# A two-part transformer block on one core: where value products, decays and root steps stand in three attention stages

## The reference, cut to what matters

```python
def mla_mixer(h, ...):                      # first attention, 8 heads, 256 tokens
    proj = h @ w_in                         # c_q 384, c_kv 256, k_pe 64
    q  = (rms_norm(c_q, q_a_norm) @ w_uq)   # 8 heads x (128 + 64)
    kv = (rms_norm(c_kv, kv_a_norm) @ w_ukv)# 8 heads x (128 keys + 128 values)
    q_nope, k_nope = rms_norm(...), rms_norm(...)        # per head
    q_pe, k_pe = rope(rms_norm(...)), rope(rms_norm(...))
    logits = (q_nope @ k_nope.T + q_pe @ k_pe.T) * scale # causal
    return softmax(logits) @ v @ w_o

def moba_mixer(h, w_qkv, ...):              # second attention, 8 heads of 128
    q, k, v = split(h @ w_qkv)
    q, k = rms_norm(q, q_norm), rms_norm(k, k_norm)      # per head
    return softmax(q @ k.T * scale + rel_bias) @ v @ w_o

def first_block(x, ...):
    x = x + mla_mixer(norm(x)); x = x + sq_relu_mlp(norm(x))
    x = x + moba_mixer(norm(x)); x = x + sq_relu_mlp(norm(x))

def hybrid_layer(x, ctx, ...):              # third stage: both halves side by side
    attn = neighbourhood_attention(q, k, v, kc, vc, rpb, rows)   # 8 heads of 64
    y    = ssd_bidirectional(...)  # decay = exp(cum_i - cum_j), masked, times C B^T dt
    x = x + gate * (concat(attn, y) @ w_out); x = x + gate * conv_glu(...)
```

## Time and profile before

| | |
|---|---|
| runs of the kernel | 1105.79, 1106.78, 1111.33 us (median 1106.78) |
| the profiled execution | 1100.91 us, of it span 1099.3 us |
| busy: PE / DVE / ACT / POOL | 94% / 64% / 48% / 9% |
| chain that ended last | PE 74%, DVE 13%, ACT 6%, issue 3%, DMA 2% |
| mean granted TensorE clock | 0.983 of 2.4 GHz |

### The profile page before, as it was taken

How to read it: one execution, slowest core, us unless ns; L and a number is a source line. 1 busy time by engine, 2 the same in 40 slices (tenths; PEclk the granted TensorE clock), 3 DMA queues, 4 the chain that set the end, 5 groups by cost and what they waited for, 6 DMA issues and landing times.

```text
span 1099.3 us, 15596 instructions
## 1 busy us (share of the span) xinstructions
PE 1036.1 (94%) x6112; PEld 886.9 (81%) x6112; DVE 703.4 (64%) x946; ACT 529.1 (48%) x712; POOL 99.2 (9%) x77
## 2 busy tenths in 40 slices
PE   7989899999999997989999999999999889999996
PEld 5556789888997875889999887988966678999995
DVE  5645556888736556557676754456477477777774
ACT  2463447766444557444554543553344255445442
POOL 0120004665000010000000000000000000000000
PEclk9997999999999999999999999999999999999998
DMA  8034466767643551547777542334100145445531
GB/s 351 1 126 104 153 232 251 274 241 272 255 158 115 191 191 44 219 159 269 280 281 283 198 184 78 115 118 151 39 1 1 43 175 200 176 172 186 200 148 57
DMA packets 29725, 183.89 MB, mean 167 GB/s; under 512 B 3440, under 2 KB 6128, under 8 KB 10096
## 3 DMA queue, kind: packets, MB, share of 16 engines
q1 hardware_dynamic: 25216, 156.84, 39.2%
q0 software_dynamic: 3456, 25.17, 6.5%
q10 hardware_dynamic: 1008, 1.27, 0.3%
HBM read 180.64 MB, written 2.62 MB: 167 GB/s over the span
## 4 chain that ended last, share of the span: by engine, by line
PE 74%; DVE 13%; ACT 6%; issue 3%; DMA 2%; POOL 1%; ACTq 0%; DVEq 0%; SPq 0%
PE bank L662 20%; PE bank L663 19%; PE bank L664 19%; DVE split L1795 4%; ACT split L1297 4%; PE bank L857 3%; PE bank L671 2%; DMA consts<-in_consts 2%; PE bank L1162 2%; PE bank L1143 1%; PE bank L945 1%; POOL stat L593 1%; PE bank L804 1%; DMA raw<-w_mlp 1%; ACT arena L1298 1%
## 5 line engine op out<-in xcount | busy, mean ns | idle before, releaser
L1795 DVE TENSOR_TENSOR split<-raw,split 128x2048 fp32r<-128x2048 f32 (+1 forms) x123 | 283.7, 2307 | 240.1 <-ACT split L1297 234.5
L1297 ACT ACTIVATE split<-raw 128x2048 fp32r<-128x2048 f32 (+1 forms) x123 | 233.6, 1899 | 267.7 <-PE bank L664 244.9
L662 PE MATMUL bank<-acts,split 128*128 128x256 f32 (+1 forms) x1024 | 290.6, 284 | 2.7 <-DVE acts L1833 1.4
L663 PE MATMUL bank<-acts,split 128*128 128x256 f32 (+1 forms) x1024 | 289.6, 283 | 0.0
L664 PE MATMUL bank<-acts,split 128*128 128x256 f32 (+1 forms) x1024 | 289.6, 283 | 0.0
L662 PE MATMUL bank<-split,acts 128*128 128x512 f32 (+1 forms) x544 | 214.4, 394 | 15.4 <-DVE split L1795 8.3
L663 PE MATMUL bank<-split,acts 128*128 128x512 f32 (+1 forms) x544 | 210.4, 387 | 0.0
L664 PE MATMUL bank<-split,acts 128*128 128x512 f32 (+1 forms) x544 | 210.3, 386 | 0.0
L662 PEld LDWEIGHTS bank<-acts,split 128*128 128x128 f32 (+1 forms) x1024 | 194.7, 190 | 6.2 <-issue 3.3
L663 PEld LDWEIGHTS bank<-acts,split 128*128 128x128 f32 (+1 forms) x1024 | 194.7, 190 | 2.3
L664 PEld LDWEIGHTS bank<-acts,split 128*128 128x128 f32 (+1 forms) x1024 | 194.7, 190 | 0.4
(11 more groups left out here) (245 smaller groups left out, 1189.6 us busy)
## 6 DMA issues: line engine op xcount, KB each, us to landing
raw<-w_mlp SPq DMA_DIRECT2D x64, 1024.0 KB, 4.9
raw<-w_glu SPq DMA_DIRECT2D x22, 1024.0 KB, 5.3
work<-w_ada POOLq DMA_DIRECT2D x12, 1024.0 KB, 5.1
raw<-w_qkv SPq DMA_DIRECT2D x12, 1024.0 KB, 4.8
bias<-w_ada POOLq DMA_DIRECT2D x12, 1024.0 KB, 5.1
arena<-w_glu_down SPq DMA_DIRECT2D x22, 512.0 KB, 3.3
raw<-w_mla_o SPq DMA_DIRECT2D x4, 1024.0 KB, 5.7
raw<-w_moba_o SPq DMA_DIRECT2D x4, 1024.0 KB, 4.8
```

What stands on the lines that cost most here:

```text
L662: pe.matmul(out_, a[0], b[0], start=first, stop=False)
L663: pe.matmul(out_, a[0], b[1], start=False, stop=False)
L1297: return act.activation(out_, in_, ACT.Copy)
L1795: v.tensor_tensor(split[:, c % 2, 1, 0:n], raw[:, c % 2, 0:n], split[:, c % 2, 0, 0:n].bitcast(F32), ALU.subtract).then_inc(lo_ready, 1)
```

## The change

What stays the same: every product, every weight byte, the four banks' turns. What changes:

1. **att0.** The four value units of `mla_ukv` are spread: one between the rotary q and the k transposes, one behind the k transposes, one behind S2, one behind O0. ACT's evictions follow (`values_out`, `beside0`). The rounded part of `mla_o` chunk 0 is made by DVE instead of ACT.
2. **Rotary keys.** `kpT` becomes two tiles of 128 rows, one with zeros in its lower and one in its upper half; L921 and L923 take 128 rows. POOL writes the zeros, ACT evicts the keys in two 64-row copies.
3. **att1.** The roots are taken in halves (q, then k; 16 columns each) and the loop covers q and k only. PE transposes q, makes value chunks 8 and 9, transposes k, makes the first half of chunk 10, S0 to S2, the other half, and chunk 11's halves behind O0 and O1. The splits of the chunks 12 and 13 (`moba_o` 0 and 1) move into and behind the attention.
4. **Third stage.** A step's segment (G, K, F) stands directly behind P, ahead of S, Y and O.

```diff
-            kpT = view(arena, 12288, T)
+            kpT = view(arena, 12288, T), view(arena, 12800, T)
@@ grid_order
         steps.append(("P", i))
+        steps.extend(x for x in SEGMENTS if SEGMENT_STEP.get(x) == i)
         ...
-        steps.extend(x for x in SEGMENTS if SEGMENT_STEP.get(x) == i)
@@ POOL
-            roots(0, 7)
+            roots(0, 3)
+            pool.wait_ge(roots_ready, 3)
+            pool.memset(kpT[0][64:128], 0.0).then_inc(kpe_zeros, 1)
+            pool.wait_ge(kpe_zeros, 1)
+            pool.memset(kpT[1][0:64], 0.0).then_inc(kpe_zeros, 1)
+            pool.wait_ge(kpe_zeros, 2)
+            roots(3, 7)
@@ PE, first attention
-            ukv_products(1)
             pe.wait_ge(heads_normed, 3)
             ...
+            ukv_products(1, 0)
             (k transposes)
+            ukv_products(1, 1)
+            def beside0(kind, h):
+                if (kind, h) == ("S", 2):
+                    ukv_products(1, 2)
+                    for u in range(4, 6):
+                        gemm_gone(pe, GU["mla_ukv"] + u)
+                if (kind, h) == ("O", 0):
+                    ukv_products(1, 3)
@@ scores0
-                pe.matmul(b[:, 0:T], qpT[a:a + 64, h // 2, P:T], kpT[a:a + 64, :], start=False, stop=True)
+                pe.matmul(b[:, 0:T], qpT[:, h // 2, P:T], kpT[h % 2][:, :], start=False, stop=True)
@@ PE, second attention
-            with pe.Fori(0, 3) as i:
+            with pe.Fori(0, 2) as i:
             ...
+            pe.wait_ge(heads_normed, 6)
+            for n in range(4):
+                heads_flip(n)
+            for c in range(2):
+                for t in range(2):
+                    value_products(c, t)
+            pe.wait_ge(heads_normed, 7)
+            for n in range(4, 8):
+                heads_flip(n)
+            value_products(2, 0)
+            def beside1(kind, h):
+                if (kind, h) == ("S", 2):
+                    value_products(2, 1)
+                    ...
+                if (kind, h) in (("O", 0), ("O", 1)):
+                    value_products(3, h)
@@ ACT
-            small_empty(SU["kpe"], kpT, T)
+            copy(kpT[0][0:64], sbank(SU["kpe"])[0:64, 0:T])
+            copy(kpT[1][64:128], sbank(SU["kpe"])[64:128, 0:T]).then_inc(small_free[SU["kpe"] % 4], 1)
-            split_hi(GC["mla_o"])
+            def beside0(h):
+                if h < 2:
+                    values_out(6 + h)
+            def beside1(h):
+                if h == 1:
+                    used(c0 + 10)
+                if h in (2, 3):
+                    values_out1(h)
+            causal_attention("att1", H, beside1)
+            used(c0 + 11)
@@ DVE
+            v.wait_ge(w_loaded[0], 16)
+            v.tensor_copy(split[:, 0, 0, :], raw[:, 0, :]).then_inc(hi_ready, 1)
             split_lo(GC["mla_o"])
@@ DVE, second attention
-            inverse_rms(8, [(32, P)])
+                    if (i, j) == (1, 1):
+                        heads_scaled(0)
+                means_of(8 + 16 * i, [(16, P)])
+            heads_scaled(1)
+            def beside1(h):
+                if h == 3:
+                    used(GC["qkv"] + 10)
```

More of the change, by code:

```diff
@@ L621, in _ @@
                 ada_load(j, att)
-            roots(8, 10)
+            roots(8, 11)
             pool.wait_ge(small_ready, SU["att1"] + 24)
@@ L626, in _ @@
                 ada_load(j, bias)
-            roots(10, 12)
+            roots(11, 13)
             for j in range(14, 24):
@@ L630, in _ @@
                 ada_load(j, bias)
-            roots(12, 13)
+            roots(13, 14)
             pool.memset(cum_rows, 0.0).then_inc(zeros_ready, 1)
@@ L638, in _ @@
             pool.wait_ge(zeros_ready, 3)
-            roots(13, len(ROOTS))
+            roots(14, len(ROOTS))
         @block.tensor
@@ L806, in t5_products, with causal_attention @@
                     ins.then_inc(small_ready, 1)
-            def causal_attention(name, scores, value, count):
+            def causal_attention(name, scores, value, count, beside):
                 for kind, h in seq_c:
@@ L825, in causal_attention @@
                             .then_inc(small_ready, 1)
+                    beside(kind, h)
             pe.wait_ge(ident_in_sb, 16)
@@ L1504, in causal_attention @@
                         transposed(h - 1)
-            causal_attention("att0", 0)
+                    beside(h)
+            def beside0(h):
+                if h < 2:
+                    values_out(6 + h)
+            causal_attention("att0", 0, beside0)
             split_hi(GC["mla_o"] + 1)
@@ L1561, in _, with values_out1 @@
                             .then_inc(gemm_free[u % 4], 1)
-            for j in range(4):
-                used(c0 + 8 + j)
-                for m in range(j - 1, j + 1) if j % 2 else ():
-                    empty(u0 + 8 + m, qkv[:, m % 2, 2048 + 512 * (m // 2):2560 + 512 * (m // 2)],
-                          scale=stat[:, m % 2:m % 2 + 1])
             for n in range(4):
                 pair_empty(SU["q1"] + n, pair(q1T, n), col("moba_q"))
+            def values_out1(n):
+                empty(u0 + 8 + n, qkv[:, n % 2, 2048 + 512 * (n // 2):2560 + 512 * (n // 2)], scale=stat[:, n % 2:n % 2 + 1])
+            used(c0 + 8)
+            used(c0 + 9)
+            values_out1(0)
+            values_out1(1)
             for n in range(4):
                 pair_empty(SU["k1"] + n, pair(k1T, n), col("moba_k"))
-            causal_attention("att1", H)
+            def beside1(h):
[5 more added lines that the diff above has]
+            used(c0 + 11)
             project_and_cols("moba_o", "m1")
@@ L1582, in _ @@
                 two_hi("hc", m, 1)
[L1583 removed]
+            norm_second_tile(14)
             used(GC["mlp1"] + 31)
@@ L2121, in _, with causal_attention @@
             scale_k_nope(1)
+            v.wait_ge(w_loaded[0], 16)
+            v.tensor_copy(split[:, 0, 0, :], raw[:, 0, :]).then_inc(hi_ready, 1)
             split_lo(GC["mla_o"])
-            def causal_attention(name, scale, bias_of, count):
+            def causal_attention(name, scale, bias_of, count, beside=None):
                 def logits(h):
@@ L2160, in causal_attention @@
                         normalise(h - 1)
+                    if beside:
+                        beside(h)
             causal_attention("att0", 1.0 / math.sqrt(NOPE + ROPE), lambda h: const("causal"), 0)
@@ L2250, in _, with heads_scaled @@
             means_of_x(2)
-            with v.Fori(0, 2) as i:
+            def heads_scaled(n):
+                v.wait_ge(roots_ready, 10 + n)
+                for u in range(4 * n, 4 * n + 4):
+                    gemm_gone(v, GU["qkv"] + u)
+                for t in range(2):
+                    qk = qkv[:, t, D * n:D * (n + 1)].rearrange("p (h d) -> p h d", d=P)
+                    at = 8 + 16 * n + 8 * t
+                    ins = v.tensor_tensor(qk, qk, spread(stat[:, at:at + 8], 1, P), ALU.mult)
+                    if t:
+                        ins.then_inc(heads_normed, 1)
+                    else:
+                        step(ins)
@@ L2252, in _ @@
+            for i in range(2):
                 for j in range(4):
-                    used(GC["qkv"] + j, i, 4)
+                    used(GC["qkv"] + 4 * i + j)
                     for m in range(j - 1, j + 1) if j % 2 else ():
-                        v.wait_ge(sq_ready, 4 * i + (11 + m))
+                        v.wait_ge(sq_ready, 4 * i + 11 + m)
                         sq = att[:, 512 * (m % 2):512 * (m % 2) + 512].rearrange("p (a b) -> p a b", a=4)
-                        v.tensor_reduce(stat[:, bass.ds(8 * i + (8 + 16 * (m % 2) + 4 * (m // 2)), 4)], sq, AX.X,
-                                        ALU.add).then_inc(sq_used, 1)
@@ L2260, in _ @@
-            used(GC["qkv"] + 8)
-            v.wait_ge(sq_used, 18)
-            inverse_rms(8, [(32, P)])
-            for u in range(8):
-                gemm_gone(v, GU["qkv"] + u)
-            for t in range(2):
-                used(GC["qkv"] + 9 + t)
-                qk = qkv[:, t, 0:2 * D].rearrange("p (h d) -> p h d", d=P)
-                ins = v.tensor_tensor(qk, qk, spread(stat[:, 8 + 16 * t:24 + 16 * t], 1, P), ALU.mult)
-                if t:
-                    ins.then_inc(heads_normed, 1)
-                else:
-                    step(ins)
+                        at = 8 + 16 * i + 8 * (m % 2) + 4 * (m // 2)
```

88 lines of the change are left out of this document (57 added, 31 removed).

## The result

| | before | after |
|---|---|---|
| runs of the pair, us | 1102.68 to 1111.33 (median 1106.28 of 4) | 1071.38 to 1077.66 (median 1075.1 of 4) |
| profiled execution / span, us | 1100.91 / 1099.3 | 1072.88 / 1071.3 |
| mean granted TensorE clock | 0.983 | 0.992 |
| busy PE / DVE / ACT | 94% / 64% / 48% | 95% / 66% / 49% |

The ratio is 0.9712, with a 95% interval of 0.966 to 0.9764: the changed kernel is faster by 31 us on this chip. Beside the experiments it was timed on two more chips: 1074.47 against 1103.18 (ratio 0.9739, interval 0.9699 to 0.9779) and 1075.03 against 1102.71 (0.9733, 0.9713 to 0.9753), so by 28 to 29 us there. 1081 was forecast, with 1074 to 1090 as range; all three medians (1075.1, 1074.47, 1075.03) lie in the range, but under the 1077 to 1084 that the prediction gave its own mechanism.

What follows compares the result with a forecast made beforehand. PE, busy 94% of the span with 74% of the chain, was taken as the bound, with idle or half-clock stretches to recover. Gains 15.8 (att0) + 7.2 (att1) + 2.9 (third stage) = 25.9 us; 1106.8 - 25.9 = 1080.9, stated 1081, range 1074 to 1090.

Steps and rivals of the forecast that it cites:

- its own mechanism: Whole kernel: the forecast's summed gains as laid out, 1081 us with own range 1077 to 1084, chance 0.55.
- the bounds 1.30 and 1.99: att0 scores per head: 1.30 us if padded to full height, 1.99 if unchanged; 1.30 was taken.
- att0's list: att0: PE's new order laid end to end from 66.9 us, projection at 100.7, gain 15.8 us.
- The waits at O0 and O1: att0: new PE waits on ACT, whose value copies stand behind exponentials, 0.6 and 0.9 us.
- The main assumption: att0: the clock is 1.00 all through, as PE has no gap over 1 us from 66.9 on.
- what preceded the fall is gone: att0: argument against the clock falling all the same; the idle 1.32 and 2.31 us are covered.
- rival B: att0: the clock falls all the same, for 17 us as before; its 8.5 us come back, 1089; chance 0.14.
- 8.5 + 3.6 + 5.5 less waits: att0 cross-check: half rate 8.5, idle time 3.6, shorter scores 5.5, less 1.5 of new waits: 16.1 us.
- The gain of 7.2: att1: PE's new list from 385.70 to the projection at 431.4, instead of 438.56; gain 7.2 us.
- The tail moves with it: Third stage: the tail, P14 on DVE on ACT on O5, moves with the stage's 2.9 us gain.
- the median of the runs is 5.9 higher: Last step: median 1106.8 against profiled 1100.9 before, so 1080.9 rather than 1075.0 is forecast.
- the low end allows for the low stretches of the slower runs going too: Range 1074 to 1090: its low end covers low-clock stretches of slower runs also disappearing.

Runs made afterwards that it cites:

- experiments 1 and 3: 1: changed kernel with one rotary key copy and 64-row rotary products, 1081.3 us. 3, first run: that kernel, second score pair turned round, 1074.69 us.
- Experiment 2: Kernel before with only the padding: rotary keys in two copies of 128 rows, no filling; 1092.41 us (ratio 0.9889).
- experiment 7: Changed kernel with waits in both attentions and the third stage attacked by order alone: 1067.93 and 1068.64 us; third stage's part alone 1070.14 us.
- the second run of experiment 3: Kernel before with only the second pair of score products in the other order, two shape changes a head instead of four; 1100.39 us (0.9976).
- short hole: Kernel before with the rounded part of the first `mla_o` chunk made on VectorE, no padding or filling; one run of 1094.75 us.
- experiment 5: Changed kernel with the third stage's order as before, segments last in their steps; 1079.56 us (0.9785).

## Why the prediction was right

**What bounds the kernel.** A stretch in which PE was busy at half clock, holes of PE in both attentions, and three waits in the third stage: each stage gave what its rows said, within 0.3 us.

**Scores.** Of the bounds 1.30 and 1.99 the lower was right, 1.31. The 0.69 was the shape, by experiments 1 and 3, and more exactly the change between shapes.

**att0's list.** S0 at 73.31 (laid at 73.0), the fourth value unit at 81.81 (81.6), P5 at 93.57 (93.8), projection at 100.48 (100.7). The waits at O0 and O1 are there with the releaser named, but 0.29 and 0.57 instead of 0.6 and 0.9; a head takes 2.29 and not 2.4, since an output product held PE for 0.65 and not the 0.76 of the earlier trace rows, which has a change of shape ahead of it too.

**The clock.** The main assumption held: 1.00 from 67.15 to 100.48. Its reason ("what preceded the fall is gone") is half of the story. Experiment 2 shows that most of what the low stretch cost, 5.1 of its 8.5 us, hung on the 64-row products (or the changes beside them) as well, which the prediction took for a matter of rate alone. Had the filling failed, the padding would have saved most of it, and rival B (1089, "as long a low stretch as before") was mispriced: a fall inside padded heads lasted 6.8 us and so costs 3.4, not 8.5. The check "8.5 + 3.6 + 5.5 less waits" came out right because either edit removes the shared part.

**Moved splits and queues.** The rounded copy on DVE took 1.23 us, near the lower bound, and ended with the subtraction at 72.2, ahead of the first logits at 74.82: zero. `mla_o` 2 was issued at 96.57; ACT began its split of that chunk at 107.81, released by PE and not by the DMA: zero, as said.

**att1.** From chunk 7's end: S0 18.5 us (forecast 18.4), P0 23.3 (23.1), P2 32.5 (32.1), P4 36.6 (36.4), projection 45.8 (45.7). S0's wait is 1.19 (0.9), O3's 0.19 (0.7). The gain of 7.2 was 7.06.

**Third stage.** 3.12 for 2.9: the three waits, and 0.2 us more. DVE waits for the outputs of a pair as foreseen, but for 5.2 us at O1 and O3 where 1 to 2 were put down, and not wholly within its slack: experiment 7 gets 0.6 us back ahead of P13 by moving `pair_lo`. "The tail moves with it" was right: P14's 2.61 stayed. It was not the fixed chain as which it was treated, though: experiment 7 removes it by moving the remainders of a pair (DVE) and one rounded pair (ACT).

**The sum and the median.** 26.2 us by the three marks against 25.9, and the forecast from the profiled execution, 1075.0, is 2.1 us over the measured 1072.88; 1.7 of these are the stretch at half clock at 860 us. The median came to 1075.1, 5.9 under the forecast and 1.9 under the forecast's own range, and the step that was off is the last one, "the median of the runs is 5.9 higher", with the same 5.9 added to the new kernel. (1 - clock) x span, averaged over the runs of a chip, is 22 to 23 us for the kernel before and 10 to 11 for the changed one. On the two chips that timed both side by side 13 and 10 us of clock loss went, not the 8.5 of att0: the other 2 to 4 us are stretches at half clock elsewhere. With them 26.2 becomes 28 to 31 us, against 28 to 29 measured on these chips and 31 on the pair's own, for which the record has no clock of the kernel before. The text allowed for such stretches in the range ("the low end allows for the low stretches of the slower runs going too") but not in the number. That the median lies in the range, 1.1 us above its lower end, is owed to this allowance; what was foreseen is the sum of the gains.

## What to carry to other kernels

Where TensorE is busy and its clock is low, look at what stands ahead of the fall (here a hole) and at what runs during it; here both could be mended, and they shared their gain. Keep products of one tile shape together, or pad the short ones with zeros, where many small products alternate. After filling a hole, list every wait that is left, ask what the releasing engine did just before, and move that: here this brought another 6 us with no new instruction.

## What the runs showed of the hardware

- A change between 64-row and 128-row float32 products costs 0.195 us at full clock (heads of 2.29, 2.68 and 3.07 us with none, two and four); the 64-row product itself costs what one of 128 rows does. At half clock a change costs 0.30 us, less than twice that (S1 to S2: 2.56, 3.15 and 3.75 us with none, two and four, in experiment 2, the second run of experiment 3 and the kernel before).
- Once the granted clock had fallen to 0.5, it stayed there for 17 us in three kernels whose next work had 64-row products among it (before, two changes, short hole), with PE shown busy all the time, and for 6.8 us in the one whose products all had 128 rows. In the other places of the kept traces, ahead of the last 15 us of the program, a low stretch lasted 3.4 or 6.8 us. With no hole ahead (experiments 1 and 3) the 64-row products never brought it down in att0.
- In one trace the fall came behind a single hole of 2.02 us ahead of the scores, and at 326 us in the changed kernel behind one of 1.70 us, with no DMA busy. Waits of 2.61 us ahead of P14 came both with a fall behind them (experiment 5, the changed kernel's third profile) and without (its first).
- Stretches of 3.4 us at half clock appear at places that differ from run to run of one program (behind att0 at about 101 us in the changed kernel's first and third profile, not in its second), and most of what separates runs is their sum: (1 - clock) x span is 8.6, 5.3 and 15.1 us in the changed kernel's three profiles, with 1072.88, 1069.37 and 1079.03 us.
